# The opening of a hybrid decoder layer on eight cores: order of norm, transposes and first projections

## What is computed

```
h = rmsnorm(x, norm_g)                       # 4096 wide
z = h @ w_in                                 # 76 column blocks of 128
u_a, gate_a, glu_val, glu_gate, gate_b, q, gate_c = split(z)
k, v = rmsnorm(mem, mem_norm_g) @ w_mem_k, w_mem_v
o_a = pool_mix(u_a) * silu(gate_a)
o_b = conv_module(glu_val * sigmoid(glu_gate)) * silu(gate_b)   # causal, width 31, layer norm, swish, pointwise
o_c = memory_attention(q, k, v) * silu(gate_c)
y = rmsnorm(x + concat(o_a, o_b, o_c) @ w_out, final_norm_g)
```

## Time and profile before

| | us |
|---|---|
| median of three runs | 1977.76 (1976.98 to 1984.7) |
| the profiled execution | 1961.31 |
| its span, first to last instruction (core 0) | 1960.0 |
| spans of the eight cores | 1936.7 to 1960.0 |
| PE busy in the span | 1841.1 (94%) |
| DVE busy | 970.0 (49%) |
| ACT busy | 355.0 (18%) |
| median span of the cores, die 0 and die 1 | 1950.9 and 1945.8 |

### The profile page before, as it was taken

The page is one execution under the profiler, slowest core; times in us unless marked ns, Lnnn a source line. Parts: engine busy times, 40 slices in busy tenths (PEclk is TensorE's granted clock), DMA queues, the critical chain, the costliest instruction groups (busy, mean ns, idle before and its releaser), DMA issues.

```text
span 1960.0 us, 29710 instructions; the slowest of 8 cores (1936.7 to 1960.0 us)
## 1 busy us (share of the span) xinstructions
PE 1841.1 (94%) x11592; PEld 927.3 (47%) x11592; DVE 970.0 (49%) x1364; ACT 355.0 (18%) x620; POOL 142.5 (7%) x270
## 2 busy tenths in 40 slices
PE   2768999999999999999999999999989999999997
PEld 1435555555544544444444555455444444444443
DVE  4548898848888888888762211111000100000455
ACT  4531111011011011011032333222000111111222
POOL 0000101110000000000000111111010000000000
PEclk9988999999999999999999999999999999999999
DMA  8853976696444444545434777888449875657898
GB/s 235 228 138 75 172 134 111 121 169 111 90 76 86 84 83 79 89 80 100 75 56 76 113 119 113 128 135 153 80 81 182 219 164 116 147 140 158 228 282 263
DMA packets 82251, 259.20 MB, mean 132 GB/s; under 512 B 12384, under 2 KB 18656, under 8 KB 76512
## 3 DMA queue, kind: packets, MB, share of 16 engines
q0 software_dynamic: 39328, 153.76, 48.6%
q1 hardware_dynamic: 42784, 103.54, 17.0%
HBM read 370.56 MB, written 40.45 MB: 210 GB/s over the span
## 4 chain that ended last, share of the span: by engine, by line
PE 84%; DMA 8%; DVE 3%; issue 2%; ACT 2%; SPq 1%; DVEq 0%; ACTq 0%; POOLq 0%
PE pz L365 74%; PE ps L365 9%; DMA y<-YF 4%; DMA wo<-w_out 1%; DMA slot<-w_in 1%; DMA XT<-x 1%; DVE HT L445 1%; SPq L1057 1%; ACT XN L426 1%; DMA slot<-w_mem_v 1%; ACT XN L421 0%; PE ps L443 0%; DMA YF<-y 0%; DVE SQ L377 0%; DVE YB L498 0%
## 5 line engine op out<-in xcount | busy, mean ns | idle before, releaser
L365 PE MATMUL pz<-HT,slot 128*128 128x512 bf16 x4864 | 1151.1, 382 | 10.3 <-DMA slot<-w_in 5.2
L387 DVE SCALAR_TENSOR_TENSOR YB<-EA,CS,YB 128x512 f32<-128x512 f32 x720 | 480.5, 744 | 0.0
L365 PEld LDWEIGHTS pz<-HT,slot 128*128 128x128 bf16 x4864 | 331.8, 98 | 314.1 <-issue 24.6
L365 PE MATMUL ps<-HT,slot 128*128 128x64 bf16 (+1 forms) x2432 | 469.6, 199 | 4.8 <-ACT SGt L371 3.6
L365 PEld LDWEIGHTS ps<-HT,slot 128*128 128x128 bf16 x2432 | 233.7, 98 | 287.7 <-issue 14.4
L377 DVE TENSOR_TENSOR YT<-pz,XR 128x512 f32<-128x512 f32 (+1 forms) x53 | 36.6, 690 | 261.5 <-PE pz L365 215.7
L341 POOL DMA_DIRECT2D slot<-w_in x152 | 81.1, 535 | 952.8 <-PE ps L365 728.5
L365 PE MATMUL pz<-wo,CCA 128*128 128x512 bf16 (+1 forms) x672 | 147.4, 382 | 0.8 <-ACT SGC L371 0.8
L365 PE MATMUL pz<-wo,CCB 128*128 128x512 bf16 (+1 forms) x672 | 145.9, 379 | 0.0
L371 ACT ACT_TABLE_LOAD x45 | 57.7, 1283 | 475.5 <-PE ps L365 241.1
L1037 ACT ACTIVATE JK<-YT 128x512 bf16<-128x512 f32 (+1 forms) x66 | 41.6, 630 | 396.8 <-DVE YT L377 396.8
(11 more groups left out here) (150 smaller groups left out, 1198.7 us busy)
## 6 DMA issues: line engine op xcount, KB each, us to landing
slot<-w_in POOLq DMA_DIRECT2D x152, 512.0 KB, 6.3
wo<-w_out POOLq DMA_DIRECT2D x32, 1024.0 KB, 17.8
XT<-x SPq DMA_DIRECT2D x8, 2048.0 KB, 13.9
XR<-x SPq DMA_DIRECT2D x64, 256.0 KB, 7.7
y<-YT SPq DMA_DIRECT2D x64, 256.0 KB, 7.9
YF<-y SPq DMA_DIRECT2D x24, 512.0 KB, 7.4
y<-YF SPq DMA_DIRECT2D x24, 512.0 KB, 9.0
slot<-w_mem_k POOLq DMA_DIRECT2D x16, 512.0 KB, 9.3
```

Source lines behind the costliest of these rows:

```text
L365: S.op("pe", lambda e: e.matmul(out, lhsT=lhsT, rhs=rhs, start=start, stop=stop), r=r, w=w, t=max(64, n) / 2400 + 0.0025)
L387: S.op("dve", lambda e: e.scalar_tensor_tensor(out=out, in0=a, scalar=s, in1=b, op0=op0, op1=op1), r=r, w=w, wa=wa, t=n / 960 + 0.13)
```

## The change

The opening and the norm are rewritten; nothing of the computation is left out.

- A third buffer XT lies where the pooling tiles lie later (R_AT + 512). Tile i uses buffer i % 3, and its load goes out when tile i-3 has been scaled.
- `norm_scale` keeps the square and the root; reciprocal and both scalings move to `norm_apply`. Both get costs on the planner's clocks that they did not have, and the eviction's goes from 1.2 to 1.33.
- `norm_transpose` takes the groups and the banks it is to use: tiles of x use banks 4 to 7 (PZ buffer 2 and both PS), one for each group, in the order 2, 3, 0, 1.
- In a step i of the opening: square and root of tile i+1, transposes 2 and 3 of tile i, scaling of tile i+1 (and the load of tile i+4), half a piece, transposes 0 and 1 of tile i, the rest of the pieces.
- A piece is one block of weights with 256 tokens (32 matmuls). Only GG 0 and V 0 are done in the opening, eight pieces in all, the first in step 3; U 0 becomes an ordinary unit behind it.
- The loads have gates: SP waits for tile 0 before it issues tile 2. POOL waits for tile 0 before weights 1 and 2, for tile 3 before weights 3 and 4, and for tile 8 before the rest.
- Memory tiles 9 and 10: their transposes stand inside the units GG 1 and V 1, after 8 and 16 of the 32 weight tiles.
- The line `S.t["dve"] = S.t["pe"]` at the end of the opening is gone.

```diff
--- before.py
+++ after.py
@@ -256,7 +256,7 @@
         HMb = [S.buf("HM%d" % i, [(R_YB + 5 * 4352 + kc * 512 + i * 256, R_YB + 5 * 4352 + kc * 512 + i * 256 + 256)
                                   for kc in range(32)]) for i in range(2)]
         KST = [at("KST", R_END, [256], F32), at("KST", R_YB + 5 * 4352 + 16384, [256], F32)]
-        XT = [at("XT", R, [D], F32), at("XT", R + 16384, [D], F32)]
+        XT = [at("XT", R, [D], F32), at("XT", R + 16384, [D], F32), at("XT", R_AT + 512, [D], F32)]
         XN, XNb = [], []
         for i, oo in enumerate((R_YB + 4352, R_YB + 3 * 4352)):
             XN.append(raw("XN", oo, [D], BF16)[0])
@@ -328,10 +328,10 @@
         free_slots = collections.deque(range(NSLOT))
         load_slot = {}
 
-        def w_fill():
+        def w_fill(limit=1 << 30):
             if recording:
                 return
-            while free_slots and wst["issue"] < len(loads):
+            while free_slots and wst["issue"] < min(limit, len(loads)):
                 k = wst["issue"]
                 wst["issue"] += 1
                 name, i = loads[k]
@@ -411,33 +411,37 @@
         S.op("dve", lambda e: e.tensor_copy(out=IDB[:], in_=IDF[:]), r=[IDFb], w=[IDb])
         S.op("dve", lambda e: e.memset(ONES[:], 1.0), w=[ONb])
 
+        landed = {}
+
         def norm_load(i, src, rows):
-            b = i % 2
-            S.dma("sp", lambda e: e.dma_start(out=XT[b][0][0:rows, :], in_=src), w=[XT[b][1]])
+            xt, xtb = XT[i % 3]
+            S.dma("sp", lambda e: e.dma_start(out=xt[0:rows, :], in_=src), w=[xtb])
+            landed[i] = list(xtb.w)
 
         def norm_scale(i, rows):
             b = i % 2
-            xt, xtb, xn, xnb, nb = XT[b][0], XT[b][1], XN[b], XNb[b], NSTb[i]
+            xt, xtb, xn, xnb, nb = XT[i % 3][0], XT[i % 3][1], XN[b], XNb[b], NSTb[i]
             S.op("act", lambda e: e.activation(out=xn[0:rows, :], in_=xt[0:rows, :], func=AF.Square, accum_out=NST[0:rows, i:i + 1]),
-                 r=[xtb], w=[xnb[0], xnb[1], nb])
+                 r=[xtb], w=[xnb[0], xnb[1], nb], t=3.6)
             S.op("act", lambda e: e.activation(out=NST[0:rows, 12 + i:13 + i], in_=NST[0:rows, i:i + 1], func=AF.Sqrt, scale=1.0 / D, bias=EPS),
-                 r=[nb], w=[nb])
-            S.op("dve", lambda e: e.reciprocal(out=NST[0:rows, 24 + i:25 + i], in_=NST[0:rows, 12 + i:13 + i]), r=[nb], w=[nb])
+                 r=[nb], w=[nb], t=0.2)
+
+        def norm_apply(i, rows):
+            b = i % 2
+            xt, xtb, xn, xnb, nb = XT[i % 3][0], XT[i % 3][1], XN[b], XNb[b], NSTb[i]
+            S.op("dve", lambda e: e.reciprocal(out=NST[0:rows, 24 + i:25 + i], in_=NST[0:rows, 12 + i:13 + i]), r=[nb], w=[nb], t=0.16)
             S.op("act", lambda e: e.activation(out=xn[0:rows, 0:2048], in_=xt[0:rows, 0:2048], func=AF.Copy, scale=NST[0:rows, 24 + i:25 + i]),
-                 r=[xtb, nb], w=[xnb[0]])
+                 r=[xtb, nb], w=[xnb[0]], t=2.0)
             S.op("dve", lambda e: e.tensor_scalar(out=xn[0:rows, 2048:4096], in0=xt[0:rows, 2048:4096], scalar1=NST[0:rows, 24 + i:25 + i],
-                                                  scalar2=None, op0=ALU.mult), r=[xtb, nb], w=[xnb[1]], t=2.2)
-
-        def norm_transpose(i, rows, gcol, dst, dstb, c0, small):
+                                                  scalar2=None, op0=ALU.mult), r=[xtb, nb], w=[xnb[1]], t=1.3)
+
+        def norm_transpose(i, rows, gcol, dst, dstb, c0, qs, banks):
             b = i % 2
-            for q in range(4):
-                if small:
-                    k = ps()
-                    t16, tb = PS16[k], PSb[k]
-                else:
-                    k = pz()
-                    t16, tb = PZ16[k], PZb[k]
-                tv = t16[:, 0:1024].rearrange("p (k n) -> p k n", k=8)
+            for q, bk in zip(qs, banks):
+                t16 = PZ16[bk // 2] if bk < 6 else PS16[bk - 6]
+                o0 = (bk % 2) * 1024 if bk < 6 else 0
+                tb = PO[bk][1]
+                tv = t16[:, o0:o0 + 1024].rearrange("p (k n) -> p k n", k=8)
                 for k in range(8):
                     kc = q * 8 + k
                     S.op("pe", lambda e, k=k, kc=kc, tv=tv: e.transpose(out=tv[:, k, 0:rows], in_=XN[b][0:rows, kc * 128:(kc + 1) * 128],
@@ -445,14 +449,27 @@
                 S.op("dve", lambda e, q=q, tv=tv: e.tensor_tensor(
                     out=dst[:, q * 8:(q + 1) * 8, c0:c0 + rows], in0=tv[:, :, 0:rows],
                     in1=CS[:, gcol + q * 8:gcol + q * 8 + 8][:, :, None].broadcast_to([128, 8, rows]), op=ALU.mult),
-                    r=[tb, CSb], wa=[dstb], t=1.2)
+                    r=[tb, CSb], wa=[dstb], t=1.33)
 
         SEGB = [HTb[0:4], HTb[4:8], HTb[8:9]]
+
+        def piece(u, p, half):
+            sl = fs[2 * u + half]
+            view = slots[sl][0][:, :].rearrange("p (k n) -> p k n", k=16)
+            for k in range(16):
+                kc = half * 16 + k
+                mm(PZ[u][:, p * 256:p * 256 + 256], view[:, k, :], HT[:, kc, p * 256:p * 256 + 256], kc == 0, kc == 31,
+                   [slots[sl][1]] + HTb[2 * p:2 * p + 2], [PZb[u]])
+
+        mid = {}
+        midn = [None]
 
         def seg_ops(sl, half, seg, lo, zi, si, rhsb):
             view = slots[sl][0][:, :].rearrange("p (k n) -> p k n", k=16)
             for k in range(16):
                 kc = half * 16 + k
+                if kc in mid:
+                    mid.pop(kc)()
                 for sg in seg:
                     if sg < 2:
                         out, a, b, tb = PZ[zi][:, sg * 512:(sg + 1) * 512], sg * 512, sg * 512 + 512, PZb[zi]
@@ -637,62 +654,83 @@
             if i < 11:
                 norm_load(i, *TILES[i])
 
-        def tile_T(i):
+        XB = (4, 5, 6, 7)
+
+        def tile_N(i):
             norm_scale(i, TILES[i][1])
+
+        def tile_A(i):
+            norm_apply(i, TILES[i][1])
             stage_load()
-            if i == 0 and not recording:
-                S.deps("pool", [XT[0][1]], [])
-                w_fill()
+
+        def tile_T(i, qs=(2, 3, 0, 1), banks=XB):
             if i < 9:
-                norm_transpose(i, TILES[i][1], C_G, HT, HTb[i], 128 * i, True)
+                norm_transpose(i, TILES[i][1], C_G, HT, HTb[i], 128 * i, qs, banks)
             else:
-                norm_transpose(i, 128, C_MG, HM, HMb[i - 9], (i - 9) * 128, False)
-
+                norm_transpose(i, 128, C_MG, HM, HMb[i - 9], (i - 9) * 128, qs, banks)
+
+        def gate(eng, i):
+            if not recording:
+                for key, val, _ in landed[i]:
+                    S._wait(eng, key, val)
+
+        first = [("in", 2 * u + h) for u in (U_GG, U_V) for h in range(2)]
+        fs = []
+
+        def tail_piece(u):
+            for half in range(2):
+                seg_ops(fs[2 * u + half], half, (2,), NPR, u, u, None)
+                w_release(fs[2 * u + half])
+
+        def weights(n, i):
+            gate("pool", i)
+            w_fill(n)
+
+        work = {3: [(0, 0)], 4: [(1, 0)], 5: [(0, 1)], 6: [(1, 1)], 7: [(0, 2)], 8: [(1, 2), (0, 3), (1, 3)]}
         stage_load()
         stage_load()
-        wp_load(0)
-        esa_load(0)
-        first = [("in", 2 * u + h) for u in (U_GG, U_V, U_U) for h in range(2)]
-        z3 = [0, 1, 2]
-        rot["pz"] = 3
-        fs = []
-
-        def first_seg(u, seg, lo, zi, si):
-            for half in range(2):
-                seg_ops(fs[2 * u + half], half, (seg,), lo, zi, si, None)
-
-        for i in range(4):
-            tile_T(i)
-        fs += [w_get(*f) for f in first]
-        first_seg(0, 0, NPR, 0, 0)
-        tile_T(4)
-        first_seg(1, 0, NPR, 1, 1)
-        tile_T(5)
-        first_seg(2, 0, NPR, 2, 0)
-        tile_T(6)
-        tile_T(7)
-        first_seg(0, 1, NPR, 0, 0)
-        tile_T(8)
+        gate("sp", 0)
+        stage_load()
+        weights(2, 0)
+        fs += [w_get(*f) for f in first[0:2]]
+        tile_N(0)
+        tile_A(0)
+        for i in range(9):
+            if i == 4:
+                weights(4, 3)
+                fs += [w_get(*f) for f in first[2:4]]
+            if i == 5:
+                wp_load(0)
+                esa_load(0)
+            if i == 8:
+                weights(6, 8)
+                gate("sp", 8)
+            todo = [(u, p, h) for u, p in work.get(i, []) for h in range(2)]
+            if i < 8:
+                tile_N(i + 1)
+            tile_T(i, (2, 3), XB[0:2])
+            if i < 8:
+                tile_A(i + 1)
+            for w_ in todo[0:1]:
+                piece(*w_)
+            tile_T(i, (0, 1), XB[2:4])
+            for w_ in todo[1:]:
+                piece(*w_)
         eus_load(0)
-        first_seg(1, 1, NPR, 1, 1)
-        first_seg(2, 1, NPR, 2, 0)
-        first_seg(0, 2, NPR, 0, 0)
-        for s_ in fs[0:2]:
-            w_release(s_)
+        tail_piece(0)
         gg_evac(0, 0, 0)
-        first_seg(1, 2, NPR, 1, 1)
-        for s_ in fs[2:4]:
-            w_release(s_)
+        tail_piece(1)
```

(19 more changed lines are left out.)

## The result

The changed kernel takes 1947.38 us (median of 4 runs, 1943.65 to 1951.29), the kernel before, beside it on the same chip, 1977.76 (median of 3); the ratio is 0.9842 [0.9812, 0.9872]. Forecast was 1946.9.

What follows compares the result with a forecast made beforehand. TensorE bounds the kernel behind the opening; DMA and each tile's lone chain bound the opening. Opening 28.5 us plus v-unit weight waits 2.4 gave 30.9: 1961.3 to 1930.4, plus 16.5 carried over, 1946.9 us; range 1934 to 1964.

Steps and rivals of the forecast that it cites:

- a slower clock: In the opening: steps 4 to 7 were charged 1 us each and the end behind tile 8 was charged 3 us.
- A planner that interleaves by estimated clocks: Behind the opening: DVE starts a further 16 us behind TensorE, and its 18 us pause by the v units covers that.

## What to carry to other kernels

Before pricing a slower clock, an order or a wait in an opening, ask what sets the pace of that stretch: under a full DMA queue they were worth 2.6 us or nothing, while a third buffer, which moves the last arrival, was worth 7 to 8 and transposes slipped inside later matmuls 15.0. A planner that interleaves by estimated clocks is part of any change ahead of it, and needs a term of its own in the sum: with the old offset between the estimates put back, the new opening gave 10 us more, and 12 us of shift alone cost the old kernel 28. Count a long wait of TensorE with the slower matmuls behind it; here that was a third of the loss. Read waits for an engine that is itself waiting through to the one behind it, and see how much each instruction behind the change finds queued ahead of it.
